# The second matrix's two-block weight sum of its sixth product by an accumulating transfer, the first matrix's by VectorE

## What is computed

```python
def reference(x, ..., w_ff1, w_ff2):
    for l in range(DEPTH):
        h = rms_norm(x, norm_mix_pre[l])
        m = hybrid_mixer(h, ...)
        x = x + rms_norm(m, norm_mix_post[l])
        h = rms_norm(x, norm_ffn_pre[l])
        f = jnp.square(jax.nn.relu(h @ w_ff1[l])) @ w_ff2[l]
        x = x + rms_norm(f, norm_ffn_post[l])
    return x
```

## Time and profile before

| | us |
|---|---|
| median of 3 runs | 973.98 |
| lowest, highest | 972.21, 975.13 |
| the profiled execution, its own time | 974.1 |
| its span in the trace | 972.4 |
| TensorE busy in the span | 955.2 (98%) |
| VectorE busy | 728.2 (75%) |
| ScalarE busy | 421.5 (43%) |
| GpSimd busy | 107.6 (11%) |
| transfers, mean | 144 GB/s |
| of them software (accumulating) ones | 26.22 MB, 15.0% of 16 engines' span |

### The profile page before, as it was taken

How to read it: one execution, slowest core, us unless ns; L and a number is a source line. 1 busy time by engine, 2 the same in 40 slices (tenths; PEclk the granted TensorE clock), 3 DMA queues, 4 the chain that set the end, 5 groups by cost and what they waited for, 6 DMA issues and landing times.

```text
span 972.4 us, 13482 instructions
## 1 busy us (share of the span) xinstructions
PE 955.2 (98%) x4878; PEld 815.9 (84%) x4878; DVE 728.2 (75%) x839; ACT 421.5 (43%) x518; POOL 107.6 (11%) x130
## 2 busy tenths in 40 slices
PE   9999999999999999999999999998999999999995
PEld 7888888888888888888888888898889989989984
DVE  5458888888888988886585444688975885895797
ACT  5333332333333322224274223466745745754762
POOL 1100001001000012113100000121102102011102
PEclk9999999999999999999999999999999999999998
DMA  6324222323322222234225323487888778888763
GB/s 244 97 88 129 94 92 92 108 92 99 104 88 89 84 87 86 91 101 134 87 96 207 118 98 122 159 213 188 244 263 166 235 210 193 233 206 227 209 191 104
DMA packets 39195, 140.21 MB, mean 144 GB/s; under 512 B 4464, under 2 KB 4592, under 8 KB 39152
## 3 DMA queue, kind: packets, MB, share of 16 engines
q1 hardware_dynamic: 30912, 110.27, 32.3%
q0 software_dynamic: 7424, 26.22, 15.0%
q10 hardware_dynamic: 816, 3.15, 0.9%
HBM read 135.43 MB, written 4.19 MB: 144 GB/s over the span
## 4 chain that ended last, share of the span: by engine, by line
PE 91%; DVE 5%; issue 2%; ACT 1%; POOL 0%; DVEq 0%; ACTq 0%; POOLq 0%
PE ps L1482 24%; PE ps L1486 24%; PE ps L1484 24%; PE ps L1645 5%; PE ps L1649 5%; PE ps L1647 5%; DVE w_lo L987 2%; DVE h_lo L987 1%; DVE wide L1338 1%; PE ps L1556 1%; PE ps L1586 1%; DVE glu L1303 1%; PE ps L1525 1%; ACT w_hi L629 1%; DVE wide L1351 0%
## 5 line engine op out<-in xcount | busy, mean ns | idle before, releaser
L1482 PE MATMUL ps<-a_hi,w_hi 128*128 128x512 f32 x576 | 225.7, 392 | 0.0
L1484 PE MATMUL ps<-a_lo,w_hi 128*128 128x512 f32 x576 | 224.2, 389 | 0.0
L1486 PE MATMUL ps<-a_hi,w_lo 128*128 128x512 f32 x576 | 224.1, 389 | 0.0
L987 DVE TENSOR_TENSOR w_lo<-raw,w_hi 128x1024 fp32r<-128x1024 f32 x124 | 153.2, 1238 | 92.4 <-ACT w_hi L629 92.0
L629 ACT ACTIVATE w_hi<-raw 128x1024 fp32r<-128x1024 f32 x124 | 130.2, 1056 | 193.4 <-PE ps L1486 119.2
L1063 DVE SCALAR_TENSOR_TENSOR conf<-glu,cols,conf (+1 forms) x240 | 186.9, 779 | 27.5 <-DVE conf L1063 26.4
L1484 PEld LDWEIGHTS ps<-a_lo,w_hi 128*128 128x128 f32 x576 | 108.2, 188 | 22.7 <-issue 0.5
L1482 PEld LDWEIGHTS ps<-a_hi,w_hi 128*128 128x128 f32 x576 | 108.1, 188 | 22.5 <-issue 0.5
L1486 PEld LDWEIGHTS ps<-a_hi,w_lo 128*128 128x128 f32 x576 | 108.1, 188 | 22.5
L987 DVE TENSOR_TENSOR w_lo<-glu,w_hi 128x1024 fp32r<-128x1024 f32 x56 | 67.7, 1222 | 34.0 <-ACT w_hi L629 30.1
L1482 PE MATMUL ps<-w_hi,h_hi 128*128 128x512 f32 x224 | 87.7, 391 | 2.8 <-DVE wide L1338 2.6
(11 more groups left out here) (167 smaller groups left out, 1615.2 us busy)
## 6 DMA issues: line engine op xcount, KB each, us to landing
raw<-units_in SPq DMA_DIRECT2D x144, 512.0 KB, 3.3
glu<-units_in SPq DMA_DIRECT2D x24, 512.0 KB, 8.0
glu<-units_in POOLq DMA_DIRECT2D x24, 512.0 KB, 7.2
raw_d<-units_in POOLq DMA_DIRECT2D x24, 512.0 KB, 5.7
raw_v<-units_in SPq DMA_DIRECT2D x16, 512.0 KB, 7.0
raw_d<-units_in SPq DMA_DIRECT2D x8, 512.0 KB, 6.5
conf<-x_in SPq DMA_DIRECT2D x4, 512.0 KB, 4.7
conf<-x_in ACTq DMA_DIRECT2D x1, 2048.0 KB, 8.1
```

Of the source, the lines that this page charges most:

```text
L987: return nc.vector.tensor_tensor(dst, src, hi, ALU.subtract)
L1482: nc.tensor.matmul(ps[:, bank, :], left_hi, right_hi, start=first, stop=False, skip_group_check=on_top)
L1484: nc.tensor.matmul(ps[:, bank, :], left_hi, right_lo, start=False, stop=False, skip_group_check=on_top)
L1486: return nc.tensor.matmul(ps[:, bank, :], left_lo, right_hi, start=False, stop=final, skip_group_check=on_top)
```

## The change

DOWN's product 7 gets its weight sum from GpSimd's accumulating transfer, as 5, 6 and 4 do. `BY_DMA` becomes a pair, one tuple for each matrix. SyncE's side load of DOWN goes, and VectorE's two `sum_beside` of DOWN. In GpSimd's queue the new transfers stand between UP 5 of the next quarter and DOWN 4. Since slots 0 and 1 are no longer read by a DOWN sum, the load of the next quarter's UP 1 waits only for the split of DOWN 1 (`w_lo_ready`) and not for a sum (`summed`).

Three more things move on VectorE. UP's sums stand earlier, ahead of the first half of product 5. `set_lo(q, "22")` stands behind product 6's work in quarter 0, and behind the split of product 6's second unit in the others. In quarter 0, `join(0, 6, "21", 0)` stands ahead of the split of product 7's second unit. In quarter 3, the two `weigh(c, 0)` move from behind product 2 to behind product 6.

```diff
-BY_DMA = (5, 6, 4)
+BY_DMA = ((5, 6, 4), (5, 6, 7, 4))
...
@@ SyncE
-                    if earlier_in_slot(u) and slot < RAW:
-                        sp.wait_ge(summed, sums_beside(q, f, h) - 2)
+                    if slot < RAW and f == DOWN:
+                        sp.wait_ge(summed, sums_beside(q, h))
                     elif earlier_in_slot(u):
                         sp.wait_ge(w_lo_ready, earlier_in_slot(u)[-1] + 1)
...
                     ff_load(q, DOWN, product)
-                side_load(q, DOWN)
@@ GpSimd
                 if q < QUARTERS - 1:
                     add_block(q + 1, UP, 5)
+                add_block(q, DOWN, 7)
                 add_block(q, DOWN, 4)
@@ ScalarE
-                if product == 7:
-                    act.wait_ge(summed, sums_beside(q, f, h))
+                if (f, product) == (UP, 7):
+                    act.wait_ge(summed, sums_beside(q, h))
                 elif product in ADDED:
                     act.wait_ge(raw_added[slot], sums_in_slot(u))
@@ VectorE
                 if q:
                     split_behind(q, UP, 2, 1)
+                    for h in range(2):
+                        sum_beside(q, h)
                 done(q, UP, 5, 0)
                 split_behind(q, UP, 5, 0)
                 if q == 0:
                     x_lo("21-22-11", 10)
+                    for h in range(2):
+                        sum_beside(q, h)
...
-                set_lo(q, "22")
-                for h in range(2):
-                    sum_beside(q, UP, h)
+                if q:
+                    set_lo(q, "22")
                 done(q, UP, 3, 0)
                 split_behind(q, UP, 3, 0)
                 if q == 0:
                     x_lo("11-21", 11)
-                done(q, UP, 3, 1)
-                split_behind(q, UP, 3, 1)
-                dve.wait_ge(kept, 5 * q + 5)
-                for h in range(2):
-                    done(q, UP, 6, h)
-                    join(q, 6, "21", h)
-                    split_behind(q, UP, 6, h)
+                if q:
+                    done(q, UP, 3, 1)
+                    split_behind(q, UP, 3, 1)
+                    dve.wait_ge(kept, 5 * q + 5)
+                    done(q, UP, 6, 0)
+                    join(q, 6, "21", 0)
+                else:
+                    dve.wait_ge(kept, 5)
+                    done(q, UP, 6, 0)
+                    join(q, 6, "21", 0)
+                    split_behind(q, UP, 3, 1)
+                split_behind(q, UP, 6, 0)
+                done(q, UP, 6, 1)
+                join(q, 6, "21", 1)
+                split_behind(q, UP, 6, 1)
+                if q == 0:
+                    set_lo(q, "22")
...
-                    if product == 3:
-                        for h in range(2):
-                            sum_beside(q, DOWN, h)
...
                     if product == 2:
                         dve.wait_ge(end_row_loaded, 16)
                         dve.wait_ge(back_loaded, 16)
-                        dve.wait_ge(mlp_sum, sums_after(q, product, 1))
+                    elif product == 6:
                         for c in (2, 3):
                             weigh(c, 0)
```

More of the change, by code:

```diff
@@ L119, in ff_loads, with side_loads, sums_beside @@
     many = sum(piece_of(v)[2] in LOADED for v in earlier_in_slot(u))
-    return 16 * (U_FF // RAW + 2 * many + 1 if ff_slot(u) < RAW else many + 1)
-def side_loads(q, f):
-    return 16 * (U_FF // RAW + 2 * (2 * q + f) + 2)
-def sums_beside(q, f, h):
-    return 2 * (2 * q + f) + h + 1
+    if ff_slot(u) >= RAW:
+        return 16 * (many + 1)
+    q, f, _, _ = piece_of(u)
+    return 16 * (U_FF // RAW + 3 * q + 2 * f + 1)
+def side_loads(q):
+    return 16 * (U_FF // RAW + 3 * q + 2)
+def sums_beside(q, h):
+    return 2 * q + h + 1
 def sums_in_slot(u):
-    return 16 * (sum(piece_of(v)[2] in BY_DMA for v in earlier_in_slot(u)) + 1)
+    return 16 * (sum(piece_of(v)[2] in BY_DMA[piece_of(v)[1]] for v in earlier_in_slot(u)) + 1)
 def source(u, added=False):
@@ L471, in ff_load, with side_load @@
                     sp.dma_start(slots[slot], units_d[source(u)]).then_inc(raw_loaded[slot], 16)
-            def side_load(q, f):
+            def side_load(q):
                 for h in range(2):
-                    sp.wait_ge(w_lo_ready, ff_unit(q, f, 1, h) + 1)
-                    sp.dma_start(slots[h], units_d[source(ff_unit(q, f, 7, h), added=True)]
+                    sp.wait_ge(w_lo_ready, ff_unit(q, UP, 1, h) + 1)
+                    sp.dma_start(slots[h], units_d[source(ff_unit(q, UP, 7, h), added=True)]
                                  ).then_inc(raw_loaded[h], 16)
@@ L486, in _ @@
                 sp.dma_start(kept_d[c * P:(c + 1) * P, :], resid[:, c, :]).then_inc(mixed_kept[c], 16)
-            side_load(0, UP)
+            side_load(0)
             def behind_sums(q, f, product):
@@ L497, in _ @@
                         ff_load(q, UP, product)
-                    side_load(q, UP)
+                    side_load(q)
                 for product in (5, 1, 2, 3):
@@ L1296, in split_behind, with sum_beside @@
                     ff_lo(u)
-            def sum_beside(q, f, h):
-                slot = slots[slot_of(f, 7) + h]
-                dve.wait_ge(raw_loaded[h], side_loads(q, f))
-                dve.wait_ge(w_lo_ready, ff_unit(q, f, 3, h) + 1)
+            def sum_beside(q, h):
+                slot = slots[slot_of(UP, 7) + h]
+                dve.wait_ge(raw_loaded[h], side_loads(q))
+                dve.wait_ge(w_lo_ready, ff_unit(q, UP, 3, h) + 1)
                 nc.vector.tensor_tensor(slot, slot, slots[h], ALU.add).then_inc(summed, 1)
```

## The result

The changed kernel takes **977.87 us** (median of 22 runs, 973.67 to 980.79), the kernel before 974.06 (22 runs, 971.95 to 978.15). The ratio is 1.0034, with a 95% interval of 1.0024 to 1.0044: slower by 3.3 us, just over what this measurement tells from no change. The profiled execution took 978.45 us, its span is 976.7, against 974.1 and 972.4. The two traces are therefore 4.3 us apart, 0.5 more than the medians and 1 more than the ratio gives. Times of the experiments were each measured beside the kernel before, and its median moved between 974.1 and 974.9 us from one to the next; so two experiments are best compared by their ratios to it.

The account below looks back on a forecast made before the run. TensorE was taken to bound the kernel, busy 955.2 of 972.4 us. Terms 3.4 + 1.5 - 0.95 - 0.4 - 1.4 sum to +2.1, so 976.2, or 976.1 against the median; range 971.0 to 979.0.

Parts of the forecast that it names:

- main case: DOWN 7's transfers late in quarter 0, the other quarters in time; 974 to 977.5 us, chance 0.50.
- the largest term: Quarter 0 up to DOWN's product 7: late accumulating transfers make TensorE start it late, +3.4 us with 0.9 from UP inside.
- UP's moved join: Quarter 0, UP 7: first half 2.8 us early, but second half still waits for the second join; gain nil.
- `set_lo` ahead of the join: Quarter 0, UP: 1.14 us of VectorE work pushes the joins and delays product 4; +0.9 us, bounds 0.7 to 1.5.
- DOWN 7 in quarter 0: Six loads and three accumulating transfers ahead delay the second landing to 713.1, product 7 to 716.3; +3.4 us including UP's 0.9.
- The clock drop there, +1.5: Quarter 0, DOWN 7: 2.7 us of idle TensorE followed by a clock drop; +1.5 us, bounds 0 and 1.7.
- Quarters 1 and 2, -0.95 and -0.4: DOWN 7's transfers land in time and waits on output sums go; quarter 1's UP join comes sooner; -0.95 and -0.4 us.
- late in other quarters too: Rival: DOWN 7's transfers also late in quarters 1 and 2; about 978.6 us, 980 with a second clock drop; chance 0.21.
- Quarter 3, -1.4: DOWN 7's 2.3 us wait goes, but moved weighings make product 4 wait 0.8; -1.4 us, bounds -0.6 to -2.3.
- Transfers in time: Rival: DOWN 7's second transfer in quarter 0 lands by 711; quarter 0 +0.6, the rest -2.75, 971.9 us; chance 0.23.

Follow-up runs that it names:

- e12: Changed kernel, in quarter 0 GpSimd issues the next quarter's two UP 5 transfers behind DOWN 4's instead of ahead of DOWN 7's; 972.95 us, ratio 0.9983.
- e13: Changed kernel, SyncE holds the next quarter's UP 1 and later loads until DOWN 7's second transfer has landed, in quarter 0 alone; 972.09 us, ratio 0.9982.
- e1: Changed kernel with VectorE's order in quarter 0's UP alone put back as it was; 977.24 us, ratio 1.0027.
- e3: Kernel before, with only DOWN 7's sum moved from VectorE to an accumulating transfer, VectorE's order otherwise as it was; 975.47 us, ratio 1.0008.
- e5: Changed kernel, in quarter 0's UP the joins moved ahead of VectorE's splits that wait for UP 4's transfers; 977.61 us, ratio 1.0037.
- e2: Changed kernel, SyncE holds the next quarter's UP 1 and later loads until DOWN 7's second transfer has landed, in quarters 0 to 2; 972.81 us, ratio 0.9976.
- e8: e7 with UP 4's two accumulating transfers issued ahead of DOWN 5's in quarter 0; 969.92 us, ratio 0.9954.
- e11: e8 with e12's edit: quarter 0 issues the next quarter's UP 5 transfers behind DOWN 4's; 973.58 us, ratio 0.9994.
- e4: Kernel before, with only VectorE's new order; DOWN 7's sums stay on VectorE with their side loads; 973.06 us, ratio 0.9987.
- e7: Changed kernel with e5's joins first and e2's hold of SyncE's loads together; 972.06 us, ratio 0.9981.

## Why the prediction was right or wrong

The forecast was 976.1 and no difference; it came out at 977.87, in the range but 0.4 above the 974 to 977.5 of its main case, and slower by a little over what can be told. The mechanism that was to be the largest term was the largest. That the sum is only 1.8 us off is in part luck, as two errors cancel: in the trace quarter 0 lost 3.5 where the terms made 4.9, and the other three lost 0.8 together where the terms gained 2.75. By its steps:

- **UP's moved join: right.** First half at 668.91 (669.1 forecast), the gain swallowed by a wait between the halves. The second half started at 674.71, not 676.5: UP 6's second accumulating transfer landed 1.5 us earlier in this execution (657.8, not 659.3), UP 4's first was issued 1.7 earlier behind it and landed at 671.7, not 673.4. Nothing in the change does that. The idle time was 2.7, not 4.5.
- **`set_lo` ahead of the join: the term of +0.9 was mis-sized, and was no constant.** Product 4 started at 680.03 (680.1 forecast). But the clock fell behind the second gap, on product 4, and UP ended 2.2 us late, above my bound of 1.5. In five kernels with this order UP ended at 683.85 to 687.30, mean 685.6; in three with the old one at 684.99 to 685.07. The move is worth +0.5 on average, with a spread of 3.4. The term rested on one landing, read in one execution.
- **DOWN 7 in quarter 0: right.** Landing at 713.0 (713.1 forecast), product 7 at 716.45 (716.3). e12 and e13 show the cause as I had it, six loads and two transfers ahead. What I did not see is that the landing stands still. In the four kernels (after, e1, e3, e5) it came 21.8 to 22.6 us behind the landing of DOWN 6's transfer, which lets the loads go, wherever between 683.1 and 687.2 UP ended. So the +0.9 did not belong beside the +2.5. The quarter ended at 727.3 in the changed kernel, whose UP was the latest, and at 728.7 to 730.3 in the three others.
- **The clock drop there, +1.5: wrong in this trace, right in three others.** After 1.71 idle us the clock stayed up. After 3.9, 5.0 and 5.3 it fell (e3, e1, e5). My 2.7 was the idle time for a UP that ends 0.9 late, and this one ended 2.2 late. The Trainium skill, TensorE: Matmul & The Clock Gate, section Why this matters for your kernels, puts the risk at idle gaps above about 3 us. The traces here do not give so sharp an edge: gaps of 2.43 and 2.74 us were followed by the lower level (e13 and e12), one of 2.94 was not (e1).
- **Quarters 1 and 2, -0.95 and -0.4: only half right.** DOWN 7's transfers were in time, and the waits on output sums went. But quarter 1 got -0.3, and quarter 2 +1.75. The failed step is that I costed the queue up to DOWN 7 and not past it: DOWN 4's transfers stand behind two more of 2.5 us each, and meet the next quarter's loads. e2 has quarters 1 and 2 at 78.4, so -1.4 and -0.6 were there to be had. I had "late in other quarters too" as a rival, at 0.21, but for DOWN 7; it was DOWN 4.
- **Quarter 3, -1.4: measured -0.7.** The 2.3 us ahead of DOWN 7 went; DOWN 4 waits 1.35 (0.8 forecast, and 0.8 to 0.9 in seven other kernels), behind the weighings and a second transfer that took 8.9 us to land. e3, with the weighings in the old place, takes 78.48 and has neither wait; the ten kernels with the transfer and the new place take 79.53 to 80.32. So the move looks like a loss of 1.1 to 1.8 us, though e3 differs in the place of UP's sums too. I had the mechanism and priced it at half.
- **Transfers in time: 971.9.** e13, in which they are, measured 972.09. The time agrees better than its terms: in e13's trace quarter 0 is 1.4 us shorter than before, where the rival had +0.6, and quarters 1 to 3 make -2.1, where it had -2.75.

## What stays open

The weighings were never put back in e8; by the table it should gain something like 1 us, which no run shows. How much of quarter 2's wait ahead of DOWN 4 is due to DOWN 7's own transfers and how much to the next quarter's loads, no run isolates. Of the 2 us between the two landings of UP 4's second transfer (673.9 and 675.8) the first half is in the packets, as the last section shows; why the second half follows is open.

## What to carry to other kernels

A wait in a queue is often a throttle as well: VectorE's sum held SyncE's loads back, and taking the sum away let four more loads, of 2 MB, run ahead of the transfer that had taken its place. When work goes from an engine to a transfer, add up the bytes that will be ahead of it from the moment the last gate opens, and go on to the transfer behind it. A landing that does not move when its issue does is the sign of this; here a gain upstream of it was worth nothing (e1, e5) until one wait on the early loads mended it.

## What was not expected of the hardware

- The time to landing of the same 512 KB accumulating transfer went from 5.1 us (alone, DOWN 7 in quarter 1) to 14.8 (e5's DOWN 4 in quarter 0) and 16.2 (e11's UP 5, behind four others).
- A packet of the instruction queue can hold a landing up. UP 4's second transfer in the changed kernel had its last data in at 673.85 us, and 15 of its 16 last packets, of 4 bytes, were through by then. Here is what moved between 673.5 and 675:

```profile
q8 instruction: 1, 0.02, 4.1%
q0 software_dynamic: 17, 0.00, 3.0%
```

  That one packet of 16 KB ran from 673.80 to 674.77; the sixteenth 4-byte packet started at 674.76, and the landing is told at 675.80. In e4 all was through at 673.60, and the landing was at 673.91. Of the 732 accumulating transfers issued behind 640 us in the 14 traces, 11 have the start of their last packet within 0.03 us of the end of such an instruction packet; those 11 landed 1.0 to 1.2 us behind it, none of the others more than 0.9. Another of the 11 is UP 6's in quarter 0 of the kernel before (659.3, where 657.8 was the changed kernel's). So by where these packets fall, a landing in quarter 0's UP is 1.5 to 2 us later in one execution than in another, whatever the edit.
- The clock. Single idle gaps followed by the lower level: 2.4 (e13), 2.5 (e7), 2.7 (e12), 2.9 (e3, e11), 3.0 (before), and all four of 3.9 and above. Not followed by it: all of 2.1 and below, and 2.4, 2.5 and 2.9 in e4, e5 and e1. Two gaps of 2.70 and 2.19, 5 us apart, had it behind the second. So between 2.4 and 2.9 both happen, and no forecast of mine should have put a whole drop or none there.
